# Conditioning rows requested after x, the function table loaded by a constant's copy, modulation weights one place later in their queue

## The reference

```python
def pool_mixer(x, w_in, w_grp, scale, w_out):        # first block
    h = x @ w_in
    u, z = h[..., :D_POOL], h[..., D_POOL:]
    ... # u minus its running mean over 2, 4, 8 or 16 tokens, one window per group of 512 columns
    m = jnp.einsum('bsgc,gcd->bsgd', m, w_grp).reshape(B, S, D_POOL) * scale
    return (m * jax.nn.silu(z)) @ w_out
x = layer_norm(DN_ALPHA * x + y, ln_g[i], ln_b[i])

silu_c, silu_cc = jax.nn.silu(c), jax.nn.silu(c_ctx)  # second block
for i in range(2):
    shift, scale, gate = jnp.split(silu_c @ w_ada[i] + b_ada[i], 3, axis=-1)
    ... # the same from silu_cc for the context
    u = h * (1.0 + scale[:, None, :]) + shift[:, None, :]
    ... # mixer A or B, then a layer norm of alpha * h + gate * y
```

## Time and profile before

| | us |
|---|---|
| median of 3 runs (2010.51 to 2013.0) | 2012.42 |
| the profiled execution | 2013.87 |
| its span | 2012.0 |
| TensorE busy in the span | 1960.5 (97%) |
| VectorE busy | 1052.8 (52%) |
| ScalarE busy | 802.6 (40%) |
| GpSimd busy | 725.9 (36%) |

### The profile page before, as it was taken

The page is one execution under the profiler, slowest core; times in us unless marked ns, Lnnn a source line. Parts: engine busy times, 40 slices in busy tenths (PEclk is TensorE's granted clock), DMA queues, the critical chain, the costliest instruction groups (busy, mean ns, idle before and its releaser), DMA issues.

```text
span 2012.0 us, 36191 instructions
## 1 busy us (share of the span) xinstructions
PE 1960.5 (97%) x14644; PEld 1627.4 (81%) x14644; DVE 1052.8 (52%) x2196; ACT 802.6 (40%) x1568; POOL 725.9 (36%) x559
## 2 busy tenths in 40 slices
PE   7999999999999999999999999999999999999996
PEld 5888888888887888888888788778888888888785
DVE  4556655865856554556665732733333333334625
ACT  3110110110125565566767620645454454555601
POOL 3333333333345822221222524562232232232545
PEclk9999999999999999999999999999999999999998
DMA  4423322232232401100111423131111111111333
GB/s 160 136 84 95 107 93 81 98 114 74 84 105 85 154 16 36 46 22 25 35 36 35 135 79 116 53 126 43 46 40 43 49 37 43 50 35 43 111 121 136
DMA packets 51044, 152.24 MB, mean 76 GB/s; under 512 B 5440, under 2 KB 11200, under 8 KB 50752
## 3 DMA queue, kind: packets, MB, share of 16 engines
q1 hardware_dynamic: 50160, 148.73, 22.3%
q10 hardware_dynamic: 720, 1.20, 0.2%
HBM read 129.20 MB, written 20.71 MB: 75 GB/s over the span
## 4 chain that ended last, share of the span: by engine, by line
PE 65%; DVE 3%; ACT 2%; issue 2%; POOL 1%; DMA 0%; DVEq 0%; SPq 0%; POOLq 0%
PE psum L935 16%; PE psum L936 15%; PE psum L937 15%; PE psum L1123 7%; PE psum L1071 6%; PE psum L1087 5%; PE psum L944 1%; POOL w_lo L758 0%; ACT u_tmp L1335 0%; DMA w_raw<-weights_in 0%; ACT u_hi L1336 0%; DVE logits L1848 0%; ACT logits L1411 0%; DVE prob_t L1870 0%; DVE u_lo L1715 0%
## 5 line engine op out<-in xcount | busy, mean ns | idle before, releaser
L935 PE MATMUL psum<-u_hi,w_hi 128*128 128x512 f32 (+1 forms) x1440 | 545.8, 379 | 3.0 <-DVE u_lo L1715 2.1
L936 PE MATMUL psum<-u_lo,w_hi 128*128 128x512 f32 (+1 forms) x1440 | 527.3, 366 | 0.0
L937 PE MATMUL psum<-u_hi,w_lo 128*128 128x512 f32 (+1 forms) x1440 | 526.7, 366 | 0.0
L756 POOL CAST w_hi<-w_raw 128x1024 fp32r<-128x1024 f32 x140 | 152.9, 1092 | 992.6 <-DMA w_raw<-weights_in 992.6
L758 POOL TENSOR_TENSOR w_lo<-w_raw,w_hi 128x1024 fp32r<-128x1024 f32 x140 | 348.0, 2486 | 11.2
L935 PEld LDWEIGHTS psum<-u_hi,w_hi 128*128 128x128 f32 x1440 | 272.6, 189 | 57.1 <-DVE u_lo L1715 3.7
L937 PEld LDWEIGHTS psum<-u_hi,w_lo 128*128 128x128 f32 x1440 | 272.8, 189 | 46.2
L936 PEld LDWEIGHTS psum<-u_lo,w_hi 128*128 128x128 f32 x1440 | 273.1, 190 | 40.2
L1411 ACT ACTIVATE logits<-logits,neg_max 128x641 f32<-128x641 f32 (+4 forms) x272 | 214.2, 788 | 58.5 <-DVE neg_max L1848 55.5
L935 PE MATMUL psum<-x_hi,w_hi 128*128 128x512 f32 x512 | 201.3, 393 | 14.9 <-DVE x_lo L1570 13.4
L1439 ACT ACTIVATE prob_t<-psum 128x320 f32<-128x320 f32 (+1 forms) x272 | 114.5, 421 | 244.0 <-PE psum L1087 243.5
(11 more groups left out here) (171 smaller groups left out, 2910.2 us busy)
## 6 DMA issues: line engine op xcount, KB each, us to landing
w_raw<-weights_in SPq DMA_DIRECT2D x140, 512.0 KB, 3.6
w_ada<-w_ada_in SPq DMA_DIRECT2D x48, 512.0 KB, 3.5
residual<-act_buf SPq DMA_DIRECT2D x4, 2048.0 KB, 7.5
res<-residual SPq DMA_DIRECT2D x26, 256.0 KB, 3.4
y_all<-staged SPq DMA_DIRECT2D x24, 256.0 KB, 4.5
act_buf<-x_t_in SPq DMA_DIRECT2D x8, 512.0 KB, 13.8
tab<-bias_tab_in SPq DMA_DIRECT2D x16, 244.5 KB, 4.5
staged<-a_y SPq DMA_DIRECT2D x6, 640.0 KB, 3.0
```

What stands on the lines that cost most here:

```text
L756: pool.tensor_copy(w_hi[:, slot, :], w_raw[:, slot, :]).then_inc(w_hi_done, 1)
L935: pe.matmul(out, wh, xh, start=first, stop=False)
L936: pe.matmul(out, wh, xl, start=False, stop=False)
L937: return pe.matmul(out, wl, xh, start=False, stop=last)
```

## The change

Three edits. First, ScalarE's list of constants loses `c_in`; it is requested on the same queue when ScalarE has made the high part of x tile 5 and x tile 7 has landed, ahead of the high part of tile 6. Second, ScalarE makes a copy of a 128x1 constant (`minus_half`, written by GpSimd) into a scratch column as its first computation. Third, in SyncE's queue the request of modulation tile n stands behind `load_unit(n + 3)`; before, it stood behind `load_unit(n + 2)`.

```diff
                 if n + W_SLOTS < A_UNIT + 2:
                     load_unit(n + W_SLOTS)
-                if n + 1 < ADA_UNITS:
-                    load_ada(n + 1)
+                if 0 < n < ADA_UNITS:
+                    load_ada(n)
...
-                 (sink_neg[:, :], bass.AP(tensor=a["sink"].tensor, offset=0, ap=[[0, P], [1, HEADS]])),
-                 (c_in[:, :, :], bass.AP(tensor=a["c_rows"].tensor, offset=0, ap=[[0, P], [D, 2], [1, D]]))]
+                 (sink_neg[:, :], bass.AP(tensor=a["sink"].tensor, offset=0, ap=[[0, P], [1, HEADS]]))]
         for dst, src in loads:
             act.dma_start(dst, src).then_inc(const_loaded, 16)
+        act.wait_ge(pool_step, 1)
+        act.activation(var_eps[:, 0:1], minus_half[:, :], ACT.Copy)
...
             act.activation(x_hi[:, k, :], act_buf[:, k, 0:S], ACT.Copy).then_inc(x_hi_done, 1)
-        act.wait_ge(const_loaded, 16 * len(loads))
+            if k == KT - 3:
+                act.wait_ge(x_loaded[KT - 1], 16)
+                act.dma_start(c_in[:, :, :], bass.AP(tensor=a["c_rows"].tensor, offset=0, ap=[[0, P], [D, 2], [1, D]])).then_inc(const_loaded, 16)
+        act.wait_ge(const_loaded, 16 * (len(loads) + 1))
```

## The result

The median went from 2012.71 us (four runs, 2010.51 to 2015.94) to 2102.74 us (four runs, 2090.4 to 2106.47). The ratio is 1.043, 95% interval 1.0402 to 1.0458: 4.3% slower. The profiled execution took 2106.47 us, its span is 2104.7.

The account below looks back on a forecast made before the run. TensorE, busy 97%, was taken to bound the kernel. Gains of -5, stalls of +64 and clock of +27 us sum to +86: 2100 us for the profiled execution, 2098 for the median, range 2062 to 2118.

Parts of the forecast that it names:

- The stalls: m and y of groups 0 to 2: modulations 7 to 12 hold VectorE, TensorE waits for banks; 21.3 us a group, 64 us.
- how long until the modulation starts: From a modulation tile's request behind a weight unit to its modulation on VectorE: 4.6 to 5.0 us, from two rows.
- The clock: TensorE's clock falls to half behind 16 of 18 new gaps, 1.7 us each: 27 us (0 to 47).
- Rival (2): Every clock restart is as long at half speed as the first, 2.6 us each: 47 us, 2118 us; chance 0.10.
- The gains: Start and first chunk of z: 3.6 us from late conditioning rows plus 1.1 us at unit 4, about 5 us.
- The copy: Table load moved off the first x tile: first matmul up to 1.28 us sooner, 0 on the path, at most 1.3.
- The gap of the third k-tile: Start: x tile 2 lands at 13.3 us, TensorE's 2.59 us gap closes; with the clock 2.6 to 4.3, taken 3.6.
- unit 4's wait: First chunk of z: unit 4 no longer queues behind modulation tile 1, so TensorE's 1.11 us wait goes.
- The rows' cover: Late conditioning rows ready at 28 to 35 us, first chunk of u at 33 to 34: 5 us cover, or 2 lost.
- (1): The stalls in groups 0 to 2 come, but TensorE's clock stays up: +59 us, 2071 us; chance 0.20.
- (3): VectorE is not away long enough to empty the banks, so only the gains stay: 2007 us; chance 0.04.
- (4): Only half of the 18 places stall, without or with the clock: 2035 to 2055 us; chance 0.07.

Follow-up runs that it names:

- late tiles only where free: The whole change, but tiles of modulations 7 to 12 of each group asked for early, as before: 2007.04 us, 0.9971 of the kernel before.
- the filled gaps: The whole change with modulation products in SBUF, plus 12 spare matmuls ahead of each of the 18 TensorE waits: 2063.33 us.
- late in y only: The whole change, but tiles 7, 8 and 9 of each group asked for early, 10 to 12 still late: 2046.14 us.
- the rows alone: The kernel before with only the conditioning rows (`c_in`) requested late, table load and tile order as before: 2007.78 us, 0.9972.
- both start edits: The changed kernel with the old modulation tile order, so only the late rows and the constant's copy remain: 2009.83 us, 0.9981.
- tile ahead of unit: The whole change, but SyncE waits for the end of unit n, then requests the modulation tile ahead of the weight unit: 2063.81 us.
- the control: The whole change with modulation products written to SBUF instead of PSUM banks 4 and 5, no spare matmuls: 2099.46 us.

## Why the prediction was right, and where its terms were off

The forecast was 2098 us, the measured median 2102.74. The mechanism held in each step: what waits behind what, which 18 modulations stall and which do not, the order of VectorE behind them, and the 5 us of gains (-5.0 by the end of z). The sum of 86 us was made of terms that were off in both directions, 6 us too much for the stalls and 9 too little for the clock; that it came within 5 us of the measured time is in part luck.

- **The stalls, 64 us (60 to 68): 58.** The step that was mis-sized is "how long until the modulation starts", 4.6 to 5.0 us from two rows. It was 4.35 to 4.7 in the changed kernel, 4.5 in the mean: 0.3 us less than the middle of my bounds in each of 18 places, and two rows are few for an amount that counts 18 times. The trace of the kernel before had two more: the tiles that were asked for behind a unit at 106.97 and 259.83 us landed after 4.4 and 4.5 us, where those of the two rows took 4.5 and 4.9. The modulation's 2.77 us (2.76 said) and the time to TensorE's restart (0.84 to 0.90, 0.84 said) held.
- **The clock, 27 us (0 to 47): 36.** The count was right (16 of 18 expected, 17 seen), the price was not: 1.7 us a gap came from single gaps with long busy stretches around them. Here the next gap is 14 us away, and a fall in y often lasted beyond 5 us (engines' busy time, then the granted clock, third from the end):

```profile
142.28:147.28 5.00, 5.00 (x22) 4.13 (x23) 1.15 (x2) 0.00 (x0) 0.00 (x0) 1.00 0.00 0
325.70:330.70 5.00, 5.00 (x12) 3.94 (x13) 0.45 (x1) 0.00 (x0) 0.00 (x0) 0.50 0.00 0
330.70:335.70 5.00, 5.00 (x22) 4.07 (x21) 1.39 (x2) 0.00 (x0) 0.00 (x0) 0.90 0.14 18
```

The rows are the time behind the restart after modulation 9 in group 0 (1.00, the one gap that left no mark) and in group 1 (0.50 for the whole of the first 5 us, 0.90 in the next 5). By the requests of weight units, a gap of y in group 1 costs 17.0 less 10.9 us, of which 3.1 are the stall: 3.0 us of clock. Rival (2), with 2.6 us each, was nearer to these than the forecast; for all 18 together the truth lay between, 2.0. In the matmul kernel of the Trainium skill ("TensorE: Matmul & The Clock Gate", HAM oscillation) every wait for a DMA between two bursts ends in a cold restart. Here the waits are for a bank, and it was so in 17 of 18 in the changed kernel, and in six of nine with three gaps a group.
- **The gains, 5 us: 5.0 in the trace up to z; 6 us in the median of the version without stalls.** The gap of the third k-tile and unit 4's wait are gone as said. The copy was put at 0, and alone it measures 0. That nothing is lost by it beside the late rows is less sure: with it the matmuls mostly stayed at half pace until 17.3 us or later, and first chunks of u came 1.1 to 2.4 us later than without it in six traces of seven. The rows' cover was wider than the bound had it: they were ready at 26.4 us, not 28 to 35.
- **Rivals.** (1), no clock, 2071, fell by the granted clock and by the filled gaps, which show what it would have been: 2063. (3), only the gains, fell with the first stall, but it is what the version with late tiles only where free does: 2007 us, as (3) had it. (4), half of the places, did not come; made on purpose (nine of them, late in y only) it gives 2046, inside its 2035 to 2055.

Two things remain open: why a fall of the clock is long in one place and short in another, and how much of the 2 us between the medians of the rows alone (2007.78) and of both start edits (2009.83) is real. In their two traces the first chunk of u is 1.5 us apart (32.94 and 34.41 us).

## What to carry to other kernels

A request moved one place later in an in-order queue is only as cheap as the distance between the new release and the use: write down, for each place of the consumer's program, which event now releases the request and how long until the data is needed. Where both hang on the same event, the whole landing time and the work behind it is exposed, and buffers cover only their own depth (here two chunks, 5.4 us, of 8.5). Count an engine that frees banks as critical for as long as it can be blocked, whatever its busy share (52% here). And when a stall of some 3 us recurs every 15 us or so, price the clock at up to the length of the stall again: here 58 us of waiting took 36 us of speed with it, in the costliest places 3.0 us beside 3.1, and spare matmuls in the gaps got the speed back but not the waiting.

## What the runs showed of the hardware that was not expected

- 216 spare matmuls made the kernel 36 us faster (2099.46 to 2063.33), with the granted clock at 1.00 in place of 0.92 over 100 to 600 us.
- Gaps of 1.7 to 2.2 us were followed by a fall of the clock in four of 15 cases (tile ahead of unit), gaps of 2.8 us and more in 42 of 48 (the changed kernel 17 of 18, the control 16 of 18, late in y only 6 of 9, tile ahead of unit 3 of 3).
- Two engines on SBUF: VectorE's 128x512 subtraction took 2.49, 2.52 and 2.55 us in the three groups of the version with the tile first, where it began behind the start of a GpSimd subtraction, and 0.69 without one; each time it ended 0.54 to 0.55 us after GpSimd's. VectorE's multiply-and-sum with one operand in PSUM kept its 1.29 us beside GpSimd's cast and the start of that subtraction. The Trainium skill ("SBUF — State Buffer", SBUF: two separate sides) has this as a lock that one of the two engines holds for a whole instruction, against VectorE instructions with two SBUF inputs; the traces agree in both cases.
